# A four-block sequence model: the first mixer's convolution shared by four engines, and norms summed in fourths

## The reference, cut to what matters

```python
h = rms_norm(x, even_norm_g)
z = h @ even_w_in + even_b_in                    # 1024 -> 2048
u, v = split(gelu(z[..., :1024]))                # 512 + 512
v = layer_norm(v, v_ln_g, v_ln_b)                # the "v" norm
ya = u * (einsum('hts,bcshd->bcthd', tril(w_s), v) + b_s)   # spatial products
a, g = split(z[..., 1024:])
c = causal_dwconv(a * sigmoid(g), conv_w, conv_b)  # 31 taps, per channel
yb = silu(layer_norm(c, conv_ln_g, conv_ln_b))     # the "conv" norm
x = x + concat(ya, yb) @ even_w_out
...
x = rms_norm(x, final_norm_g)                    # the "final" norm
# second block, two layers, twice in each:
h = layer_norm_2(alpha * h + ..., ln_g, ln_b)    # ln1_0, ln2_0, ln1_1, ln2_1
```

## Time and profile before

| | |
|---|---|
| median of three runs | 2489.47 us |
| profiled execution | 2488.94 us |
| its span in the trace | 2487.2 us |
| around the span | 1.74 us |
| granted clock of PE, mean | 0.988 |
| PE, PEld | 2403.3 us (97%), 1925.8 us (77%) |
| DVE, ACT, POOL | 1410.2 us (57%), 1077.8 us (43%), 125.5 us (5%) |
| first mixer | 0 to about 207 us |
| ln1_0, ln2_0, ln1_1, ln2_1 begin | 1450, 1818, 2096, 2464 us |
| final norm | 1180 to 1189 us |

### The profile page before, as it was taken

The page is one execution under the profiler, slowest core; times in us unless marked ns, Lnnn a source line. Parts: engine busy times, 40 slices in busy tenths (PEclk is TensorE's granted clock), DMA queues, the critical chain, the costliest instruction groups (busy, mean ns, idle before and its releaser), DMA issues.

```text
span 2487.2 us, 33162 instructions
## 1 busy us (share of the span) xinstructions
PE 2403.3 (97%) x11908; PEld 1925.8 (77%) x11908; DVE 1410.2 (57%) x2270; ACT 1077.8 (43%) x1673; POOL 125.5 (5%) x115
## 2 busy tenths in 40 slices
PE   8989999999999999999899989999989998999997
PEld 6657888887887888888777768888868776888885
DVE  5877777436775677732538764234353777532434
ACT  4444444325885444422437543233253673422422
POOL 0001000010000000000400010000113001000000
PEclk9999999999999999999999999999999999999999
DMA  4112232222121322222221122322222112222222
GB/s 176 61 43 93 93 101 93 97 98 77 59 67 60 102 93 100 94 95 100 99 69 35 60 68 93 102 93 99 96 98 77 44 35 76 85 93 100 94 94 76
DMA packets 57438, 210.63 MB, mean 85 GB/s; under 512 B 6478, under 2 KB 6880, under 8 KB 56960
## 3 DMA queue, kind: packets, MB, share of 16 engines
q1 hardware_dynamic: 56736, 204.51, 24.4%
q0 software_dynamic: 608, 4.81, 0.5%
HBM read 207.20 MB, written 2.10 MB: 84 GB/s over the span
## 4 chain that ended last, share of the span: by engine, by line
PE 72%; issue 19%; DVE 4%; POOLq 2%; ACT 1%; POOL 1%; DVEq 0%; DMA 0%; SPq 0%; ACTq 0%
PE PS L1160 13%; PE PS L1162 13%; PE PS L1161 13%; PE PS L1188 9%; PE PS L1190 9%; PE PS L1189 9%; PE PS L1219 1%; DVE CONV L1832 1%; DVE RSTD L1771 1%; POOLq L582 1%; PE PS L1274 1%; PE PS L1370 1%; POOLq L591 1%; PE PS L1358 1%; POOLq L552 1%
## 5 line engine op out<-in xcount | busy, mean ns | idle before, releaser
L1160 PE MATMUL PS<-HH,WH 128*128 128x512 f32 x1792 | 708.6, 395 | 7.1 <-DVE KR L2012 4.5
L1757 DVE TENSOR_TENSOR WL<-RAW,WH 128x1024 fp32r<-128x1024 f32 x376 | 476.0, 1266 | 421.8 <-ACT WH L610 420.2
L1162 PE MATMUL PS<-HH,WL 128*128 128x512 f32 x1792 | 699.2, 390 | 0.0
L1161 PE MATMUL PS<-HL,WH 128*128 128x512 f32 x1792 | 698.9, 390 | 0.0
L610 ACT ACTIVATE WH<-RAW 128x1024 fp32r<-128x1024 f32 x376 | 397.8, 1058 | 694.4 <-PE PS L1190 411.0
L1160 PEld LDWEIGHTS PS<-HH,WH 128*128 128x128 f32 x1792 | 337.1, 188 | 83.7 <-issue 8.0
L1161 PEld LDWEIGHTS PS<-HL,WH 128*128 128x128 f32 x1792 | 337.2, 188 | 71.8 <-issue 3.6
L1162 PEld LDWEIGHTS PS<-HH,WL 128*128 128x128 f32 x1792 | 336.9, 188 | 71.4
L1190 PE MATMUL PS<-MH,WL 128*128 128x512 f32 x864 | 336.2, 389 | 0.0
L1189 PE MATMUL PS<-ML,WH 128*128 128x512 f32 x864 | 336.2, 389 | 0.0
L1188 PE MATMUL PS<-MH,WH 128*128 128x512 f32 x864 | 336.2, 389 | 0.0
(11 more groups left out here) (291 smaller groups left out, 2588.7 us busy)
## 6 DMA issues: line engine op xcount, KB each, us to landing
RAW<-wstream SPq DMA_DIRECT2D x376, 512.0 KB, 3.2
W<-cmp_w POOLq DMA_DIRECT2D x2, 2048.0 KB, 8.2
X<-xt SPq DMA_DIRECT2D x4, 512.0 KB, 6.5
out<-X SPq DMA_DIRECT2D x8, 256.0 KB, 2.0
TAB<-tables SPq DMA_DIRECT2D x1, 1871.5 KB, 13.1
WS<-spatial_w SPq DMA_DIRECT2D x1, 512.0 KB, 8.8
BS<-spatial_b SPq DMA_DIRECT2D x1, 256.0 KB, 9.2
PW<-pool_w POOLq DMA_DIRECT2D x2, 128.0 KB, 2.4
```

Of the source, the lines that this page charges most:

```text
L1160: pe.matmul(PS[:, bank, :], WH[:, b, w], HH[:, k, :], start=(k == 0), stop=False)
L1161: pe.matmul(PS[:, bank, :], WH[:, b, w], HL[:, k, :], start=False, stop=False)
L1162: last = pe.matmul(PS[:, bank, :], WL[:, b, w], HH[:, k, :], start=False, stop=(k == DC - 1))
L1757: dve.tensor_tensor(WL[:, b, :], RAW[:, b, :], WH[:, b, :].bitcast(F32), ALU.subtract).then_inc(w_lo, 1)
```

## The change

1. **Convolution.** Chunk 0 gets its first seven taps (`AHEAD` = 7) on DVE after `step(2)` (4) and `step(3)` (3); then chunks 0 and 1 alternate, chunk 0 seven ahead. Both accumulate in PSUM (banks 4 and 5); only the last tap writes `CONV`. Chunk 3 has 10 taps on PE instead of 31 (`DIAG` = 10); ACT adds the bias to bank 7 in place, and DVE does the other 21 taps there: four pairs with chunk 1 around the v norm's waits, three more pairs, then 14 alone. Chunk 2 leaves DVE: ACT makes one product per tap (`products`, 4 ahead of the last sigmoid, 4 behind each gelu of v, 4, 4 and 3 behind those of tiles 12 to 14) into a ring of five buffers, and POOL adds them to `CONV`, 30 additions, each waiting for the last. ACT waits for POOL before it reuses a buffer of the ring.
2. **Order.** The diagonals are all made after the first gelu of v. The turn of V and the spatial products use banks 2, 3, 4, 6; the turn waits for chunk 0's last tap. `mix_y(0)` stands ahead of the last tap, and ACT's `y_high(0)` ahead of the squares.
3. **Norms in fourths** (v, final, ln1_0 to ln2_1). The sum of squares is made by four products per chunk, each with 32 columns of ones and 128 tokens, into four groups of 32 partitions. Root and reciprocal then cover 128 x 128 instead of 128 x 512. `widen` spreads the result to all partitions with four products of 128 x 128 in PSUM, and DVE multiplies straight from there. The last norm's full-row `RSTD` is no longer made.

The core of the diff:

```diff
+DIAG = 10
+RING, RING_AT = 5, 3
+CONV_BANK = {0: 4, 1: 5, 3: 7}
+TURN_BANK = (2, 3, 4, 6)
+AHEAD = 7
...
+            for k in range(1, TAPS):
+                pool.wait_ge(e_prod, k + 1)
+                if k > 1:
+                    pool.wait_ge(e_tap, k - 1)
+                pool.tensor_tensor(CONV[:, 2, :], CONV[:, 2, :], Y[:, RING_AT + k % RING, :], ALU.add).then_inc(e_tap, 1)
...
+                cols = slice(0, P if nm in WIDE else T)
+                act.activation(STD[:, cols], PS[:, bank, cols], ACT.Sqrt, scale=1.0 / width, bias=eps).then_inc(n_std, 1)
...
+            def products(first, last):
+                for k in range(first, last):
+                    src, w = CB[:, 2, k:k + T], vec("even_conv_w", 2 * TAPS + k)
+                    if k == 0:
+                        act.wait_ge(e_glu, 3)
+                        ins = act.activation(CONV[:, 2, :], src, ACT.Identity, scale=w, bias=vec("even_conv_b", 2))
+                    else:
+                        if k > RING:
+                            act.wait_ge(e_tap, k - RING)
+                        ins = act.activation(Y[:, RING_AT + k % RING, :], src, ACT.Copy, scale=w)
+                    ins.then_inc(e_prod, 1)
...
+                if j == HC - 1:
+                    products(0, 4)
...
+                if j == 0:
+                    for k in range(DIAG):
+                        ins = act.activation(TAPD[:, k, :], tab("identity"), ACT.Identity,
+                                             scale=vec("even_conv_w", (HC - 1) * TAPS + k))
+                    ins.then_inc(e_diag, 1)
+                products(4 + 4 * j, 8 + 4 * j)
...
+            def sum_quarters(src, bank, ready, first, final):
+                pe.wait_ge(*ready)
+                for q in range(TT):
+                    last = pe.matmul(PS[q * QUARTER:(q + 1) * QUARTER, bank, 0:P], tab("ones")[:, 0:QUARTER],
+                                     src[:, q * P:(q + 1) * P], start=first, stop=final)
...
+            def widen(nm, bank):
+                pe.wait_ge(n_inv, WIDE[nm])
+                for q in range(TT):
+                    pick = tab("pick")[:, q:q + 1].to_broadcast([P, P])
+                    last = pe.matmul(PS[:, bank, q * P:(q + 1) * P], pick, STD[:, P:2 * P], start=True, stop=True)
...
-            taps(0)
+            taps(0, 4)
             sum_rows(V, 2, [(n, e_gelu, n + 1) for n in range(HC)], n_add)
+            taps(4, DIAG)
             tile(12)
...
             tile(13)
-            taps(1)
+            widen("v", 6)
             tile(14)
+            pe.wait_ge(e_conv[0], TAPS)
...
-            taps(2)
             tile(15)
...
+                    ins = dve.scalar_tensor_tensor(CONV[:, n, :] if k == TAPS - 1 else acc, src, w, acc, ALU.mult, ALU.add)
...
-                taps = (0, 0, 0, 0, 3, 2, 2, 2, 2, 3, 2, 3)[s]
+                if s in (2, 3):
+                    first_chunk((0, 4)[s - 2], (4, AHEAD)[s - 2])
+                taps = (0, 0, 0, 0, 2, 2, 2, 2, 2, 2, 2, 1)[s]
...
-            two_chunks(done + 7, done + 9)
-            spread("v", RSTDV)
+            two_chunks(done + 7, TAPS - AHEAD)
+            dve.wait_ge(e_kept3, 1)
+            late_chunks(0, 2)
+            invert_quarters("v")
+            late_chunks(2, 4)
+            dve.wait_ge(n_wide, WIDE["v"])
...
-            third_chunk(0, 22)
+            last_chunk(DIAG + AHEAD, DIAG + AHEAD + 4)
             step(15)
-            third_chunk(22, TAPS)
+            last_chunk(DIAG + AHEAD + 4, TAPS - 1)
             dve.wait_ge(s_loaded, 32)
-            mean(6, HALF, n_add, 2 * HC)
+            mix_y(0)
+            last_chunk(TAPS - 1, TAPS)
+            mean(5, HALF, n_add, 2 * HC)
             centre(CONV, range(HC))
```

More of the change, by code:

```diff
@@ L144 @@
     _at += _w
+WIDE = {n: i + 1 for i, n in enumerate(["v", "final"] + [f"ln{a}_{l}" for l in range(DEPTH2) for a in (1, 2)])}
+QUARTER = 32
 ROWS, _at = {}, 0
@@ L390, in program @@
         e_gelu = sem("e_gelu")
-        e_conv = sem("e_conv")
+        e_conv = {n: sem(f"e_taps{n}") for n in (0, 1, 3)}
+        e_prod = sem("e_prod")
+        e_tap = sem("e_tap")
         e_diag = sem("e_diag")
@@ L678, in _ @@
                 gelu(s)
[L679 to L682, removed]
+                if j == 0:
[4 more added lines that the diff above has]
+                products(4 + 4 * j, 8 + 4 * j)
             squares(NB, V, range(HC), n_cent, 0)
+            act.wait_ge(e_conv3, 1)
+            act.activation(PS[:, 7, :], PS[:, 7, :], ACT.Identity, bias=vec("even_conv_b", HC - 1)).then_inc(e_kept3, 1)
             split_hi(0, 14)
             gelu(12)
+            products(20, 24)
             bring_root("v")
@@ L1265, in tile, with taps @@
                 project(0, s)
[L1267 to L1276, removed]
+            def taps(first, last):
+                pe.wait_ge(e_glu, HC)
+                pe.wait_ge(e_diag, 1)
+                for k in range(first, last):
+                    ins = pe.matmul(PS[:, 7, :], TAPD[:, k, :], CB[:, HC - 1, k:k + T], start=(k == 0), stop=(k == DIAG - 1))
+                    if k == DIAG - 1:
+                        ins.then_inc(e_conv3, 1)
             for s in range(1, 12):
                 tile(s)
-            taps(0)
+            taps(0, 4)
             sum_rows(V, 2, [(n, e_gelu, n + 1) for n in range(HC)], n_add)
+            taps(4, DIAG)
             tile(12)
             for n in range(HC):
-                sum_squares(NB, n, 3, "v", n == HC - 1)
+                sum_quarters(NB[:, n, :], 3, (n_sq, NORM["v"][0] + n + 1), n == 0, n == HC - 1)
             tile(13)
-            taps(1)
+            widen("v", 6)
             tile(14)
+            pe.wait_ge(e_conv[0], TAPS)
             for t in range(TT):
@@ L1443, in _ @@
             conv_ffn(1)
-            sum_last(2, NBF[:, 0, :], NBF, n_sq, NORM["final"][0], "final", n_sum)
+            sum_quarters(NBF[:, 0, :], 2, (n_part, PART["final"]), True, False)
+            sum_quarters(NBF[:, DC - 1, :], 2, (n_sq, NORM["final"][0] + DC), False, True)
+            widen("final", 3)
             def layer_norm(nm):
@@ L1450, in layer_norm @@
                 for n in range(DC):
-                    sum_squares(NB2, n, 3, nm, n == DC - 1)
+                    sum_quarters(NB2[:, n, :], 3, (n_sq, NORM[nm][0] + n + 1), n == 0, n == DC - 1)
+                widen(nm, 2)
             def mix_layer(l):
@@ L1772, in spread, with invert_quarters, spread_wide @@
                 dve.drain()
+            def invert_quarters(nm):
+                dve.wait_ge(n_std, NORM[nm][1] + 1)
+                dve.reciprocal(STD[:, P:2 * P], STD[:, 0:P]).then_inc(n_inv, 1)
+            def spread_wide(nm):
+                invert_quarters(nm)
+                dve.wait_ge(n_wide, WIDE[nm])
             def rows(buf, src, gain, fill):
@@ L2092, in _ @@
             split_lo(0, L_IN[0] + 1)
-            spread("final")
+            spread_wide("final")
             rows(X, X, "final_norm_g", H_FILL["in0"])
@@ L2101, in layer_norm @@
                     split_lo(0, slot)
-                spread(nm)
+                spread_wide(nm)
                 gain, bias = nm.replace("_", "_g"), nm.replace("_", "_b")
```

73 lines of the change are left out of this document (41 added, 32 removed).

## The result

The changed kernel took 2467.32 us (median of four runs, 2466.05 to 2467.80) against 2489.39 us of the kernel before (four runs, 2488.27 to 2490.13). The ratio is 0.9912, with a 95% interval of 0.9898 to 0.9925. The prediction was 2466.5 us. The profiled execution has a span of 2464.3 us where before had 2487.2, so 22.9 us are to be found in the two traces. One of the 16 executions of the kernel before that the first four experiments are compared with took 3487.65 us at a granted clock of 0.651; it is left out, and the median of the other 15 is 2487.37 us.

A forecast was written before the change was run, and what follows sets the result against it. PE bounds nearly everywhere; the change saves where PE waits, in the first mixer and norms. 8.7 + 13.2 + 1.0 = 22.9 us off 2488.94 gives 2466.0, median 2466.5; forecast 2462.5 to 2470 (0.51), wider range 2457 to 2477.

The forecast's parts named there:

- the layout: First mixer: four engine queues in code order with POOL excluding DVE; last tap 8.0 us sooner, stage end 8.7.
- The end of the stage: First mixer: last tap about 7.2 us sooner; behind it `mix_y(0)` out of the way gives 1.4, other waits take back 0.6.
- DVE's work: First mixer up to the last tap: chunks moved, early taps into waits, shorter reciprocal, `mix_y(0)` ahead; -14.1 us in sum.
- Held by POOL: First mixer: POOL's additions delay one `glu` 0.8, five or so `split_lo` 4.0, three centrings of V 3.3; +8.1 us.
- Rival 1: First mixer: POOL hardly holds DVE, stage gains 13 us instead of 8.7, kernel 2462, or 2458 with high clock; chance 0.17.
- Waits: First mixer, DVE: all waits together 11.1 us before, 9.9 after, -1.2; the early taps' -4.6 was counted under DVE's work.
- seven early taps: First mixer: seven taps of chunk 0 go into DVE's waits of 3.06 and 2.40 us and just fit; -4.6 us.
- Both bounds: First mixer, taps into PSUM: 0.60 us apart (stage about -11), or 0.80 with dependent ones 1.04 (-2.2); taken as unchanged.
- rival 2: First mixer: taps in PSUM 0.80 us apart, or additions at 2.0 us (stage -3.6); kernel 2472 us; chance 0.18.
- Norms: Four layer norms of the second block: sums -2.4, root -0.3, reciprocal and spread -0.5 to -1.4; 3.3 us each, 13.2 together.
- rival 3: Norms: fourths do not overlap, or switching the product's shape costs as much; each norm gains 0.9 us, kernel 2476; chance 0.07.
- Rival 4: First mixer: POOL becomes the bound; kernel slower from additions of 2.94 us on, 2493 us at 3.16; chance 0.03.

The follow-up runs named there:

- the first four experiments: Norms alone on the kernel before, 2473.79 us; mixer alone, 2479.62; changed kernel with POOL's additions on 128 of 512 columns, 2460.66; changed kernel with taps' sums in SBUF, 2483.33.

## Why the prediction was right

The sum was 8.7 + 13.2 + 1.0 = 22.9 us, and the traces have 8.6 and 14.0 with 0.8 of luck at the start and 0.4 lost in between. The mechanisms are those named; the terms have errors of their own that partly cancel. The 8.7 of the stage was the layout's figure: the terms of the list alone give 7.2 and 0.8, which is 8.0.

- *The end of the stage.* Last tap: -7.5 us counted from the piece's start, where the sum said -7.2 and the layout -8.0; behind it -1.1 more, predicted -0.8. The first `add_rows` started at 153.93 (said 153 to 155), slot 18's split at 163.52.
- *DVE's work.* From the start of the piece to the last tap DVE's waits, the brackets of its timeline, went from 15.7 to 10.9 us (-4.9) and what POOL holds is 6.7, so the work itself fell by 9.3. The prediction's figure, -14.1 with the 4.6 that are waits and not work taken out, is -9.5.
- *Held by POOL.* Said 8.1, measured 6.7: 0.75 at one `glu`, 3.1 at four `split_lo` (not five), 2.9 at the centring. The addition's length was said 1.36 and is 1.45. The experiments bear the term out: all 6.7 are gone when the additions are short, of which 5.4 reach the end of the piece, and 17.5 are lost when the taps collide too. Rival 1 falls.
- *Waits.* Said -5.8 in all (-4.6 and -1.2), measured -4.9. The waits at the last `glu` and at slot 11 are 1.94 and 2.75, said 2.1 and 3.0; that these come from ScalarE's order was shown by changing it. But the 4.6 us credited to the seven early taps as a step of its own was too much: undone, they cost 1.6 in the stage, and 3.0 by the medians. What they fill is in part filled by something else when they go. It did no harm to the sum because the term of the waits was laid out with them in place.
- *PSUM.* A tap has 747 ns, as in SBUF, 0.66 us apart (8 in 5.35) and 0.79 when dependent (9 in 7.08). Both bounds and rival 2 fall. The estimate by the Trainium skill, "VectorE: DVE Perf Modes", on the TRN2 errata, 5 us for 83 taps, isn't borne out: no row shows anything of the 62 cycles for a PSUM source. The Trainium skill, "GPSIMD Engine Reference", Specifications, has contention with POOL for DVE instructions with two SBUF inputs; the 6.88 us for four taps against 2.72 agree.
- *Norms.* Said 3.3 each, measured 2.9, 3.2, 4.1 and 3.0, and 13.6 us for all five when they were changed alone, where the sum had 14.2. That the four add up to the 13.2 foretold is in part luck: at the low clock that was assumed for all, a norm gives 2.9, and ln1_1 at the high one makes up for it. Sums: the root starts 0.77 us behind the last square, so the fourths do overlap, and rival 3 falls. (The product with 64 columns in the earlier trace rows that the prediction took its 57 ns from is one of the spatial weights, not of ones; the reading held all the same.) Reciprocal 0.95, as said. From the end of the last square to the first product it is 5.9 us in ln1_0, said 5.5: 0.1 of it is the root's start, and 0.2 is `widen`, since from the reciprocal to DVE's next instruction it is 3.13 us where I had allowed 0.95 and 1.95. At the high clock I had 4.1 and ln1_1 has 4.1.
- *Final norm.* Said 1.0, measured 0.8; its reciprocal does wait for `split_lo` as before.
- *Rival 4* had no share: POOL ended at 136.9 us, before the last tap, and even the slowest row of additions, 7 in 11.47 (the last of four; 16 in 25.77 are 1.61 each), has 1.64 each, far from 2.94.

## What to carry over

When a vector engine and the general engine share work, look at each instruction's operands before its length: here one operand moved from SBUF to PSUM decided whether 30 additions next door cost 7 us or 24. What a step that fills a wait is worth can't be read off that wait alone; lay the queues out without it and see what fills the hole. And where the matrix engine waits before a short product on the critical path, read the granted clock of that stretch: cheap products of the same shape in the wait bought 1.1 us for each norm that stood at the low clock, those of another shape cost as much as they brought.

## What I had not expected of the hardware

- The clock of one and the same norm differs between kernels that do not differ there. Of the 27 norms (ln1_0, ln2_0 and ln1_1) in nine kernels in fourths and without fillers, 19 took 11.5 us, six 10.3 and two 10.55 and 10.72. What decides it wasn't found; with fillers of the sums' own shape in PE's waits, all six of two kernels took 10.34.
- A change of the product's shape, from 32 to 128 columns and back, costs PE time: a sum of 8 records with 32 columns takes 0.24 us up to the next of its kind and 0.35 up to a full product, and a full product of 2 records takes 0.42 up to the small ones, where some 0.22 are usual between full ones (10 records in 1.28 with the last one's end).
- The first tap, a multiply and add of one tensor with two scalars, took 808 ns into PSUM (L1893, two instructions) where its neighbours with three inputs took 747. It costs nothing here.
